# A float32 decoder block on one core: the second feed-forward product done in seven block products, its weight sums made in DRAM

## The reference, cut to what matters

```python
def swiglu_ffn(x, g, w_in, w_out):
    h = rmsnorm(x, g)
    gate, up = jnp.split(h @ w_in, 2, axis=-1)
    return x + (jax.nn.silu(gate) * up) @ w_out      # w_out: 2816 x 1024
...
    return rmsnorm(x, g_final)
```

## Time and profile before

| | |
|---|---|
| time, median of 3 runs | 898.3 us (898.12 to 898.41) |
| profiled execution, its own time | 898.53 us |
| its span | 896.8 us |
| PE busy | 886.3 us (99%), 5292 matmuls |
| DVE, ACT, POOL busy | 595.5, 385.5, 57.6 us |
| DMA | 108 MB, mean 121 GB/s |

### The profile page before, as it was taken

One profiled execution on the slowest core, in us unless ns is written; L12 is line 12 of the kernel. 1 busy time (PEld: TensorE's weight loads), 2 busy tenths in 40 slices (PEclk: granted clock), 3 DMA queues, 4 the chain that ended last, 5 costly groups with the idle time before them and its releaser, 6 DMA issues.

```text
span 896.8 us, 13165 instructions
## 1 busy us (share of the span) xinstructions
PE 886.3 (99%) x5292; PEld 791.8 (88%) x5292; DVE 595.5 (66%) x711; ACT 385.5 (43%) x555; POOL 57.6 (6%) x59
## 2 busy tenths in 40 slices
PE   8999999999999999999999999999999999999997
PEld 7998888889999999988888788899999999888886
DVE  5685666699577678755466476998888887433333
ACT  5654432346444444533253332554555455322223
POOL 0111000000000000035100063000000000000000
PEclk9999999999999999999999999999999999999999
DMA  9946332212422232662211023123322232322212
GB/s 342 365 177 252 124 105 94 95 48 94 142 86 103 95 102 88 247 269 94 94 48 55 41 95 121 67 95 105 129 94 94 94 124 110 118 94 94 94 48 94
DMA packets 16091, 108.17 MB, mean 121 GB/s; under 512 B 1840, under 2 KB 1968, under 8 KB 4016
## 3 DMA queue, kind: packets, MB, share of 16 engines
q1 hardware_dynamic: 13408, 93.99, 28.6%
q10 hardware_dynamic: 2176, 12.00, 3.5%
q0 software_dynamic: 464, 1.57, 0.5%
HBM read 101.26 MB, written 6.29 MB: 120 GB/s over the span
## 4 chain that ended last, share of the span: by engine, by line
PE 90%; DVE 5%; ACT 2%; issue 1%; DMA 1%; ACTq 0%; POOLq 0%; POOL 0%; DVEq 0%
PE psum L1445 30%; PE psum L1446 30%; PE psum L1447 30%; DMA pack<-first 1%; DVE tl L870 1%; DVE wl L870 1%; ACT wh L395 0%; PE psum L1697 0%; ACT pr L683 0%; PE psum L1497 0%; PE psum L1824 0%; DVE w7l L870 0%; DVE sm L1215 0%; DVE hn L1290 0%; DVE gt L1280 0%
## 5 line engine op out<-in xcount | busy, mean ns | idle before, releaser
L1445 PE MATMUL psum<-th,w7h 128*128 128x256 f32 x504 | 142.7, 283 | 0.3 <-ACT snap L395 0.3
L1447 PE MATMUL psum<-th,w7l 128*128 128x256 f32 x504 | 142.6, 283 | 0.0
L1446 PE MATMUL psum<-tl,w7h 128*128 128x256 f32 x504 | 142.6, 283 | 0.0
L870 DVE TENSOR_TENSOR wl<-raw,wh 128x2048 fp32r<-128x2048 f32 (+1 forms) x44 | 89.4, 2043 | 49.1 <-ACT wh L395 49.0
L1445 PEld LDWEIGHTS psum<-th,w7h 128*128 128x128 f32 x504 | 96.7, 192 | 0.5 <-issue 0.5
L1446 PEld LDWEIGHTS psum<-tl,w7h 128*128 128x128 f32 x504 | 96.8, 192 | 0.0
L1447 PEld LDWEIGHTS psum<-th,w7l 128*128 128x128 f32 x504 | 96.8, 192 | 0.0
L395 ACT ACTIVATE wh<-raw 128x2048 fp32r<-128x2048 f32 (+1 forms) x44 | 73.1, 1676 | 20.7 <-PE psum L1447 19.6
L1445 PE MATMUL psum<-hh,wh 128*128 128x512 f32 x192 | 75.0, 391 | 0.0
L1447 PE MATMUL psum<-hh,wl 128*128 128x512 f32 x192 | 74.7, 389 | 0.0
L1446 PE MATMUL psum<-hl,wh 128*128 128x512 f32 x192 | 74.7, 389 | 0.0
(11 more groups left out here) (265 smaller groups left out, 2195.0 us busy)
## 6 DMA issues: line engine op xcount, KB each, us to landing
raw<-weights SPq DMA_DIRECT2D x79, 1024.0 KB, 4.8
pack<-first SPq DMA_DIRECT2D x3, 768.0 KB, 8.5
vraw<-weights SPq DMA_DIRECT2D x2, 1024.0 KB, 12.7
xt<-xt SPq DMA_DIRECT2D x1, 2048.0 KB, 19.5
X<-x SPq DMA_DIRECT2D x2, 1024.0 KB, 28.2
X<-x ACTq DMA_DIRECT2D x1, 2048.0 KB, 10.2
memt<-memt SPq DMA_DIRECT2D x1, 1024.0 KB, 23.2
kv_store<-kh ACTq DMA_DIRECT2D x1, 1024.0 KB, 3.9
```

What stands on the lines that cost most here:

```text
L870: return V.tensor_tensor(dst, v, f32(hi), ALU.subtract)
L1445: nc.tensor.matmul(dst, lh, rh, start=start, stop=False, **kw)
L1446: nc.tensor.matmul(dst, lh, rl, start=False, stop=False, **kw)
L1447: return nc.tensor.matmul(dst, ll, rh, start=False, stop=stop, **kw)
```

## The change

**The algebra.** For ten of the eleven pairs the product is cut in two by two blocks: tokens into halves of 256 (`Q`), hidden units into the pair's two blocks, output columns into halves of 512. The result is then built from seven block products in place of eight. Each block product is `out_product` (a block of 256 tokens, in two tiles `m`, by 512 columns): two times `mm3`, 6 matmuls with 512 columns. The eleventh pair stays plain: 48 matmuls. The products of one kind are summed over all ten pairs in PSUM, two banks each. Seven kinds need fourteen banks, so there are two passes over the ten pairs: the first makes P1, P5 and P6 (banks 4 to 7, 0 and 1), the second P2, P3, P4 and P7 (all eight banks). Between and behind the passes, partial results are copied to SBUF (`kept`) by ACT and added to banks by DVE (`merge_part`). The residual goes to two banks at the second pass's start, the other six through PSUM to SBUF (`xres`) during the first pass and from there into the sums.

**Operands.** Each pass splits its own operands anew: in the first, three weight blocks of 512 columns and 256 + 512 columns of hidden values (one is a difference) a pair; in the second, four weight blocks and 512 + 512 columns. The sums of hidden values are made by DVE in place, two operations of 256 columns a pair and pass.

**Weight sums.** The sums of weight blocks are made in DRAM, in a new tensor `fo_sums`, by transfers that POOL issues after the load of `wgr`: per pair one copy of four blocks (1 MB), one adding transfer onto three blocks (0.75 MB) and one adding transfer of two blocks onto two others (0.5 MB). They go in twelve steps; each step issues up to three transfers, of three different pairs, and POOL then waits until all have landed.

**Loads.** SP loads a pair's blocks for each pass in two transfers, one from the weights and one from `fo_sums`, into four slots, `raw` and the new `more`: 20 loads of 0.75 or 1 MB and one for the eleventh pair, where 11 of 1 MB stood.

Some semaphores of other stages are merged into one (`rstd_ready`, `squares_ready`, `var_ready`, `token_sums`); the waits stand where they stood.

```diff
@@ sync
-            with sp.Fori(K0 // 2 + 1, PANELS // 2) as i:
+            with sp.Fori(K0 // 2 + 1, FO0 // 2) as i:
...
+            for q in range(2 * NP + 1):
+                if q < 2:
+                    sp.wait_ge(lo_ready, FO0 + q - 1)
+                elif q < 4:
+                    sp.wait_ge(panel_done, FO0)
+                else:
+                    sp.wait_ge(lo_ready, FO0 + q - 3)
+                if q == 0:
+                    sp.wait_ge(fo_made, 16 * 3 * NP)
...
+                sp.dma_start(dst, src).then_inc(piece_here[q % 4], 16)
+                if q < 2 * NP:
+                    src = fo_sums[q % NP, :, 0:2, :] if q < NP else fo_sums[q % NP, :, 2:4, :]
+                    sp.dma_start(fo_raw(q)[:, 0:2 * S], src.rearrange("p b c -> p (b c)")).then_inc(fo_sum[q % 4], 16)
@@ gpsimd
             pool.dma_start(wgr[:], wg_in).then_inc(wg_here, 16)
+            made = 0
+            for step in range(NP + 2):
+                if step < NP:
+                    pool.dma_start(fo_sums[step], fo_in[step, :, 0:4 * S].rearrange("p (b c) -> p b c", b=4)).then_inc(fo_made, 16)
+                    made += 16
+                if 1 <= step <= NP:
+                    q = step - 1
+                    pool.dma_start(fo_sums[q, :, 1:4, :], fo_in[q, :, 3 * S:6 * S].rearrange("p (b c) -> p b c", b=3),
+                                   accum_op=ALU.add).then_inc(fo_made, 16)
+                    made += 16
+                if step >= 2:
+                    q = step - 2
+                    pool.dma_start(fo_sums[q, :, 0:4:2, :], fo_sums[q, :, 1:4:2, :], accum_op=ALU.add).then_inc(fo_made, 16)
+                    made += 16
+                pool.wait_ge(fo_made, made)
@@ scalar
+            def first_pass_hi(i):
+                p = i % SLOTS
+                act.wait_ge(hid_ready, 2 * i + 2)
+                act.wait_ge(panel_done, FO0 + i - 1)
+                copy(hsh[p][:, 0, 0:Q], hid[:, 2 * i, 0:Q]).then_inc(hid_first_hi, 1)
+                act.wait_ge(*fo_landed(i, 1))
+                copy(foh[p][:, 2 * S:3 * S], fo_raw(i)[:, 2 * S:3 * S]).then_inc(fo_first_hi, 1)
+            def first_pass_sums_hi(i):
+                p = i % SLOTS
+                act.wait_ge(token_sums, i + 5)
+                copy(flat(hsh[p])[:, Q:Q + S], hid[:, 2 * i, :]).then_inc(hsh_ready, 1)
+                act.wait_ge(*fo_landed(i, 2))
+                copy(foh[p][:, 0:2 * S], fo_raw(i)[:, 0:2 * S]).then_inc(hi_ready, 1)
...
+            for i in range(1, NP):
+                first_pass_hi(i)
+                first_pass_sums_hi(i)
+                if 3 <= i < 9:
+                    keep_residual(i - 3)
@@ vector
+            def first_pass_lo(i):
+                p, w = i % SLOTS, fo_raw(i)
+                dve.wait_ge(hid_first_hi, i + 1)
+                lo(hsl[p][:, 0, 0:Q], hid[:, 2 * i, 0:Q], hsh[p][:, 0, 0:Q]).then_inc(hid_first_lo, 1)
+                chain(V.tensor_tensor(hid[:, 2 * i, Q:S], hid[:, 2 * i, Q:S], hid[:, 2 * i + 1, Q:S], ALU.subtract))
+                V.tensor_tensor(hid[:, 2 * i, 0:Q], hid[:, 2 * i, Q:S], hid[:, 2 * i, 0:Q], ALU.subtract).then_inc(token_sums, 1)
...
@@ tensor
+            for i in range(NP):
...
+                out_product(4, p, 0, 2, start=i == 0, signal=done)
+                pe.wait_ge(hsl_ready, i + 1)
+                pe.wait_ge(lo_ready, FO0 + i + 1)
+                out_product(6, p, 2, 1, start=i == 0, signal=done)
...
+                out_product(0, p, 1, 0, start=i == 0, signal=done, closing=True).then_inc(panel_done, 1)
...
+            pe.wait_ge(lo_ready, FC0 + 1)
+            pe.wait_ge(hsl_ready, 2 * NP + 1)
```

More of the change, by code:

```diff
@@ L283, in small, with fo_raw, fo_landed, part_done @@
             return sm[:, i:i + n]
+        def fo_raw(q):
+            return raw[:, q % 4, :] if q % 4 < 2 else more[:, q % 4 - 2, :]
+        def fo_landed(q, steps=1):
+            return (piece_here[q % 4], 16 * (q // 4) + (48 if q % 4 < 2 else 32)) if steps == 1 else (fo_sum[q % 4], 16 * (q // 4) + 16)
+        def part_done(product, m):
+            if m == 1 and product in ("P6", "P7"):
+                return panel_done, FB0 if product == "P6" else FC0
+            return fo_part, {"P1": 0, "P5": 2, "P6": 4, "P2": 5, "P3": 7, "P4": 9, "P7": 11}[product] + m + 1
+        def out_bank(t, half):
+            return bank[((4, 6), (5, 7), (2, 0), (3, 1))[t][half]]
         def pack_part(i):
@@ new lines, in keep_part @@
+            def keep_part(which, product, src):
+                for m in range(2):
+                    act.wait_ge(*part_done(product, m))
+                    copy(kept[:, which, m, :], bank[src + m]).then_inc(fo_kept, 1)
+            act_window(NS - 1, 1, None, more=False, early=(lambda: first_pass_hi(0), lambda: first_pass_sums_hi(0)))
+            strassen_silu(1, NS - 1)
+            for i in range(1, NP):
[3 more added lines that the diff above has]
+                    keep_residual(i - 3)
@@ L1271, in _ @@
             dve.wait_ge(res_sums, 2)
-            V.tensor_scalar(small(GV, TT), bank[4][:, 0:TT], 1.0 / D, EPS, ALU.mult, ALU.add).then_inc(res_var, 1)
+            V.tensor_scalar(small(GV, TT), bank[4][:, 0:TT], 1.0 / D, EPS, ALU.mult, ALU.add).then_inc(var_ready, 1)
             split_lo(FI0 + 1)
@@ new lines, in out_product @@
+            def out_product(banks, p, a, w, start=False, signal=None, free=None, closing=False):
+                h, g = hsh[p][:].rearrange("p a b -> p (a b)"), hsl[p][:].rearrange("p a b -> p (a b)")
+                c = slice(w * S, (w + 1) * S)
+                for m in range(2):
+                    if free:
+                        pe.wait_ge(free[0], free[1] + m)
+                    r = slice(a * Q + m * P, a * Q + (m + 1) * P)
+                    ins = mm3(bank[banks + m], h[:, r], g[:, r], foh[p][:, c], fol[p][:, c], start, signal is not None, skip_group_check=True)
+                    if signal and not (m == 1 and closing):
+                        ins.then_inc(signal, 1)
+                return ins
@@ new lines, in _ @@
+            pe.wait_ge(lo_ready, FC0 + 1)
+            pe.wait_ge(hsl_ready, 2 * NP + 1)
+            order = (4, 5, 6, 7, 2, 0, 3, 1)
+            for t in range(TT):
+                for half in range(2):
+                    dst = ((4, 6), (5, 7), (2, 0), (3, 1))[t][half]
+                    pe.wait_ge(fo_merged, 2 + order.index(dst) + 1)
+                    for k in range(2):
+                        w = (half, 2 + half)[k]
+                        c, r = slice(w * S, (w + 1) * S), slice(t * P, (t + 1) * P)
+                        ins = mm3(bank[dst], hsh[0][:, k, r], hsl[0][:, k, r], foh[0][:, c], fol[0][:, c], False, k == 1, skip_group_check=True)
+                    if (t, half) == (TT - 1, 1):
+                        ins.then_inc(panel_done, 1)
+                    else:
+                        ins.then_inc(fo_tile, 1)
```

323 lines of the change are left out of this document (215 added, 108 removed).

## The result

| | before | changed kernel |
|---|---|---|
| median, us (4 runs each, same chip) | 898.21 (898.08 to 898.41) | 886.7 (886.24 to 886.87) |
| ratio, 95% interval | | 0.9871 (0.9859 to 0.9883) |
| profiled execution: own time / span, us | 898.53 / 896.8 | 886.68 / 884.7 |

The forecast was 886.0 us, with a range of 885.0 to 892.0. The kernel became 11.5 us faster by the medians, 12.1 by the two spans, where the sum said 12.5.

What follows compares the result with a forecast made beforehand. PE, busy 99% of the span, was taken to bound the kernel. Terms -13.6 + 0.4 + 0.5 + 0.2 = -12.5 us, from the profiled 898.53, gave 886.0 us, range 885.0 to 892.0.

Steps and rivals of the forecast that it cites:

- The matmuls: Second feed-forward product: 468 matmuls for 528, 60 fewer at 0.2266 us, 13.6 us less if PE never waits.
- The bank that changes every 3 matmuls: PE's result bank changes every 3 matmuls instead of 6; taken at nothing, 2.8 us if each of 140 changes cost 0.02.
- The three waits: PE waits in the second product: 0.4 us at entry, 0.5 between the passes, 0.2 ahead of the plain pair.
- the plain pair's: Ahead of the eleventh pair: DVE's last split ends at 5.57 us, PE is through at 5.44; 0.2 us wait.
- Feeding the first pass: First pass: DVE's sequence with ACT takes 4.0 us a pair against PE's 4.08; no wait in the middle.
- the loads of the third and fourth pairs: First pass: loaded only after 767.7 us, two landings giving 777; taken at nothing, 1 us kept.
- feeding is tighter: Rival, first pass: 0.5 us more in each of ten pairs and 1 us of loads, 888.5 to 892; chance 0.14.
- The sums in DRAM: POOL's transfers during the gates: adding counted twice, 35 MB; 282 us allowed, 205 expected, so no cost.
- POOL's term: Time of POOL's transfers from 124 us: 205 us, ending at 329; 145 or 320 under other costs of adding.
- The latest start of the sum of squares: POOL's next work, 21 us when packed, could start at 406 us without being late.
- The loads beside them: Panel loads in the gates: PE waits only if landings exceed 11.1 us for long; 7.7 expected, no cost.
- The rival in which POOL is late: First attention panel: POOL ends at 444 us, 38 after 406, PE waits for `res_acc`, 924 us; chance 0.06.

Runs made afterwards that it cites:

- swap: Changed kernel with ACT and DVE splitting the weight blocks in the other order for the second pass's first pair; 885.89 us.
- feed1: Changed kernel with one more unused DVE operation of 256 columns in each first-pass pair from the second on; 886.33 us.
- no_sums: Changed kernel without POOL's thirty transfers, SP loading plain weight blocks of the same size in place of the sums; 886.49 us, ratio 0.9870.
- dose6: Changed kernel with POOL's steps repeated for six more pairs (18 more transfers) into a tensor nobody reads; 896.05 us, one run.
- flood: Changed kernel with POOL's twelve steps replaced by ten copies at once, then ten first adds, then ten second adds; 887.35 us, ratio 0.9884.
- dose10: Changed kernel with POOL's steps repeated for ten more pairs (30 more transfers) into a tensor nobody reads; 947.36 us, one run.
- all3: Changed kernel with other split order at the second pass's start, residual halts two pairs earlier and the eleventh pair split early; 885.68 us.

## Why the prediction was right

**The matmuls.** 60 went, at 0.2266 us: 13.6 us. (The row at 873.99 isn't the last pair's first matmul: that pair has 48 and starts at 880.11, and the 75 reach back into the pair before. The pace over them is as stated.) The bank that changes every 3 matmuls costs nothing; the steps stay at 0.227. From the stage's start (767.52 before, with its first transposes, 767.59 after) to the last matmul it took 123.24 us before, 111.10 after: 12.14 less, which is 13.6 - 1.4 within 0.1 and the whole difference of the spans. Of the 0.7 us by which the profiled execution, 886.68, lies above the forecast, 0.3 are the waits, and 0.25 lie outside the span (2.0 us around it, where the sum took 1.7).

**The three waits.** 0.4 / 0.5 / 0.2 were forecast, 0.47 / 0.54 / 0.38 measured, 1.4 for 1.1. Each sits at its forecast place. The first two rows name DVE's split of `fol` as releaser; the third names none, but DVE's split of `hsl` ended 0.10 us before PE went on. The mis-sized term is the plain pair's: DVE's last split ended at 867.85 while PE came to it at 867.66, 0.2 us as forecast, but PE started 0.10 after the split's end, and the step behind it was 0.31 in place of 0.227, which adds 0.08. The same slow step is in the 0.47 of the first wait. Behind the eight transposes it stands without a wait too (0.31 in `swap`), so it is no part of the 0.54.

**Feeding the first pass.** DVE's steps in a pair are 0.33, 0.45, 0.35, 1.73 and 1.14 us, 4.00 in sum, where 0.32, 0.5, 0.41, 1.65 and 1.13 were added up to 4.0. No wait stands in the middle of the pass, as forecast, and the loads of the third and fourth pairs cost nothing. The rival "feeding is tighter" was wrong in one point that I could have seen: in my sum ACT, not DVE, sets the 1.65, and that leaves DVE idle time that `feed1` used up.

**The sums in DRAM.** The conclusion held: they cost nothing that the time shows, by `no_sums`. The size of POOL's term was off, 166 us (124.2 to 289.7, where the next issue of `dose6` follows the last landing) for 205, inside its bounds of 145 to 320. Counting an adding transfer twice was somewhat too much: 1.7 by `flood`. By `flood`'s rates the moving alone is an estimated 10 x 4.1 + 12.5 x 6.9 = 127 us, where 160 was taken; the 39 left for landings and issues are near the 44 taken. With 282 us allowed, the miss had no weight. The latest start of the sum of squares, 406 by estimate, stands: in `dose10` the packed sums took 18.2 us (468.04 to 486.27), in `dose6` 23.6, and PE wants them at 429.1, so 405.5 to 411. `dose6` began them at 410.65 and was late by 2.9 us, PE itself having come 2.4 us later.

**The loads beside them.** 11.5 us was the longest, 0.4 above the bound, and PE's 192.00 busy us in the gates stayed whole. With the same transfers the longest was 12.4 in `all3`, and PE lost 0.7 us: the cost of nothing was right for this profile, with less margin than its median suggests. The Trainium skill (DMA: Bandwidth & Descriptors, on queues and rings) has the DMA engines take turns between queues packet by packet, by which the prediction had put a load at 7.7 us. That estimate fits the medians beside the stepped transfers from 124 to 290 us, 7.1 here and 7.2 to 8.0 in eight other kernels that have them. It doesn't fit the longest landings (10.9 to 12.4 in the nine), the later steps of `dose6` (9.9 from 290 to 410 us), or the full queue of `flood` (10.4), where a load keeps less than half.

**What it missed.** The rival in which POOL is late was priced one for one. Its place and start were right, but it left out the clock, which added 3.2 us behind a halt of 2.9 and 3.6 behind the long one. On the 38 us of that rival it would have been an estimated tenth more.

## What to carry to other kernels

Time an idle queue and an idle stretch of DMA before putting preparatory work there: here 30 transfers, 166 us, made nothing late on POOL because the queue's next duty lay 98 us further on, and 121 us more of the same work cost 9 us (one run). Look at the longest landings beside it in several executions, not at the median of one. When two engines feed a third in turns, add up both chains: a feed that looks full may hold slack behind the other engine. Read a wait of PE from the distance of two starts against the pace, and count the slow step behind it.

## What the runs showed of the hardware that I had not expected

- In the second product, after each of the three halts and after each group of transposes, the first matmul lasted 0.47 or 0.48 us in place of 0.39, and the step behind it was 0.31 or 0.32 in place of 0.227.
- After a halt of 2.7 us (`dose6`) the granted clock was 0.51 for 7 us, and matmuls came every 0.427 us; that cost 3.2 us, nearly the same as after the halt of 56 us in `dose10` (3.6). The halt of 1.8 us in `dose6` left the clock at 1.00 (328 to 336 us).
- An adding transfer between DRAM tensors took 1.7 times a copy's time per byte (6.9 against 4.1 us a MB), and POOL 0.84 to 1.20 us to issue, against some 0.55.
- A POOL operation of 512 columns took 1.04 us in `dose10`, where all engines stood. Twice in `dose6` it took 2.97 us, both times beside a split of 2048 columns on DVE, which itself took 3.36 and 2.52 in place of 2.29.
